# The activations' two halves placed behind the weights' slots and the constants in a partition of SBUF

## What is computed

```python
mod = silu(c) @ w_ada + b_ada                  # six vectors of 2048
hn = modulated_rms_norm(h, sh1, sc1)
proj = hn @ w_in                               # 2048 x 5664: attention q/k/v, DeltaNet q/k/v, z, b, a
attn_out = axial_gqa_attention(...)            # 8 heads, 2 kv heads
dn_out = bidir_gated_deltanet(...)             # 8 heads, chunks, both directions
h = h + gt1 * (concat(attn_out, dn_out) @ w_out)
hn = modulated_rms_norm(h, sh2, sc2)
u = dwconv_centred(hn @ w_up, w_ffn_conv) + b_ffn_conv      # 2048 x 11264
h = h + gt2 * ((silu(u_gate) * u_val) @ w_down)             # 5632 x 2048
return rms_norm(h) * final_norm
```

## Time and profile before

| | |
|---|---|
| median of 3 runs | 2742.33 us (2741.33 to 2742.73) |
| the profiled execution's own time | 2742.49 us |
| its span, first to last instruction | 2739.5 us |
| TensorE: matmul instructions busy | 2580.1 us of the span, 12198 instructions |
| VectorE / ScalarE busy | 1430.4 us / 1018.2 us |
| mean granted TensorE clock | 0.977 |

### The profile page before, as it was taken

How to read it: one execution, slowest core, us unless ns; L and a number is a source line. 1 busy time by engine, 2 the same in 40 slices (tenths; PEclk the granted TensorE clock), 3 DMA queues, 4 the chain that set the end, 5 groups by cost and what they waited for, 6 DMA issues and landing times.

```text
span 2739.5 us, 35454 instructions
## 1 busy us (share of the span) xinstructions
PE 2580.1 (94%) x12198; PEld 2093.2 (76%) x12198; DVE 1430.4 (52%) x1846; ACT 1018.2 (37%) x1422; POOL 189.5 (7%) x270
## 2 busy tenths in 40 slices
PE   2589999999999989997999999999999999999997
PEld 1467877878778768785888888887888888888885
DVE  5835666666666654445444434444344444444554
ACT  4124343343443443434444234443234432222334
POOL 2200211211211201100000000000000000000000
PEclk9689999999999999999999999999999999999998
DMA  9835434445445422432333333333333333333233
GB/s 338 299 106 155 139 111 143 138 115 146 131 116 151 132 62 70 123 98 59 96 92 90 95 106 92 95 97 90 97 96 99 92 90 94 100 100 99 85 90 123
DMA packets 436095, 318.42 MB, mean 116 GB/s; under 512 B 12582, under 2 KB 408657, under 8 KB 435537
## 3 DMA queue, kind: packets, MB, share of 16 engines
q1 hardware_dynamic: 406192, 212.19, 27.0%
q0 software_dynamic: 28928, 104.87, 12.0%
q10 hardware_dynamic: 929, 0.74, 0.1%
HBM read 313.56 MB, written 4.19 MB: 116 GB/s over the span
## 4 chain that ended last, share of the span: by engine, by line
PE 85%; DVE 6%; ACT 3%; DMA 3%; issue 2%; DVEq 0%; ACTq 0%; POOLq 0%
PE pw L1307 22%; PE pw L1309 21%; PE pw L1308 21%; PE pw L1291 2%; PE pw L1292 2%; PE pw L1293 2%; PE pd L1525 2%; PE pd L1548 1%; PE pd L1561 1%; DMA DD<-in_w_ada_dram 1%; DMA T<-in_w_ada_dram 1%; PE pd L1508 1%; PE pd L1568 1%; DVE act L1014 1%; DVE PTb L864 1%
## 5 line engine op out<-in xcount | busy, mean ns | idle before, releaser
L1307 PE MATMUL pw<-act_hi,w_hi 128*128 128x512 f32 x2048 | 832.9, 407 | 17.2 <-DVE act_lo L1202 9.2
L848 DVE TENSOR_TENSOR w_lo<-raw,w_hi 128x1024 fp32r<-128x1024 f32 x426 | 520.6, 1222 | 548.1 <-ACT w_hi L502 546.4
L1309 PE MATMUL pw<-act_hi,w_lo 128*128 128x512 f32 x2048 | 800.7, 391 | 0.0
L1308 PE MATMUL pw<-act_lo,w_hi 128*128 128x512 f32 x2048 | 798.7, 390 | 0.0
L502 ACT ACTIVATE w_hi<-raw 128x1024 fp32r<-128x1024 f32 x426 | 450.3, 1058 | 526.4 <-PE pw L1309 440.8
L1307 PEld LDWEIGHTS pw<-act_hi,w_hi 128*128 128x128 f32 x2048 | 385.7, 188 | 112.0 <-issue 23.3
L1309 PEld LDWEIGHTS pw<-act_hi,w_lo 128*128 128x128 f32 x2048 | 385.2, 188 | 83.2
L1308 PEld LDWEIGHTS pw<-act_lo,w_hi 128*128 128x128 f32 x2048 | 386.3, 189 | 78.6 <-issue 7.2
L1307 PE MATMUL pw<-mh_hi,w_hi 128*128 128x512 f32 x704 | 280.3, 398 | 1.1 <-DVE w_lo L848 1.1
L1308 PE MATMUL pw<-mh_lo,w_hi 128*128 128x512 f32 x704 | 278.3, 395 | 0.0
L1309 PE MATMUL pw<-mh_hi,w_lo 128*128 128x512 f32 x704 | 278.3, 395 | 0.0
(11 more groups left out here) (265 smaller groups left out, 2562.0 us busy)
## 6 DMA issues: line engine op xcount, KB each, us to landing
raw<-in_w_up_dram SPq DMA_DIRECT2D x176, 512.0 KB, 4.1
ada_w<-in_w_ada_dram POOLq DMA_DIRECT2D x128, 512.0 KB, 4.4
raw<-in_w_in_dram SPq DMA_DIRECT2D x88, 512.0 KB, 3.9
raw<-in_w_down_dram SPq DMA_DIRECT2D x64, 384.0 KB, 3.5
raw<-in_w_down_dram SPq DMA_DIRECT2D x64, 320.0 KB, 3.2
raw<-in_w_out_dram SPq DMA_DIRECT2D x32, 512.0 KB, 4.4
DD<-in_w_ada_dram POOLq DMA_DIRECT2D x16, 512.0 KB, 6.0
EG<-in_w_ada_dram POOLq DMA_DIRECT2D x16, 512.0 KB, 5.4
```

The source lines that it names most:

```text
L848: V.tensor_tensor(w_lo[slot][:], raw[slot][:], w_hi[slot][:].bitcast(F32), ALU.subtract).then_inc(lo_made.sem, 1)
L1307: M(bank, w_hi[slot][:, k, :], hi[:, k0 + k, :], start=first, stop=False)
L1308: M(bank, w_hi[slot][:, k, :], lo[:, k0 + k, :], start=False, stop=False)
L1309: ins = M(bank, w_lo[slot][:, k, :], hi[:, k0 + k, :], start=False, stop=last)
```

## The change

The lines that allocate `act_hi`, `x_feat`, `otok` and `act_lo` are moved from the front of the list to behind `nrm`. Nothing else is edited: on each of the five engines the program has the same instructions in the same order.

```diff
-        act_hi = sb("act_hi", [P, KT, S], F32R)
-
-        for_float32 = ExitStack()
-        x_feat = sb("x_feat", [P, KT, S], F32, for_float32)
-        for_float32.close()
-        otok = sb("otok", [P, NB, DM], F32, for_float32)
-        for_float32.close()
-        act_lo = sb("act_lo", [P, KT, S], F32R)
         raw = [sb(f"raw{i}", [P, UK, P]) for i in range(2)]
         w_hi = [sb(f"w_hi{i}", [P, UK, P], F32R) for i in range(2)]
         w_lo = [sb(f"w_lo{i}", [P, UK, P], F32R) for i in range(2)]
...
         nrm = sb("nrm", [P, 3, NB])
+        act_hi = sb("act_hi", [P, KT, S], F32R)
+
+        for_float32 = ExitStack()
+        x_feat = sb("x_feat", [P, KT, S], F32, for_float32)
+        for_float32.close()
+        otok = sb("otok", [P, NB, DM], F32, for_float32)
+        for_float32.close()
+        act_lo = sb("act_lo", [P, KT, S], F32R)
```

## The result

The changed kernel takes 2777.16 us (median of 4 runs, 2774.8 to 2779.2), the kernel before 2741.83 us in the same comparison: ratio 1.013, 95% interval 1.0116 to 1.0144. It is 35.3 us slower. The profiled execution has a span of 2774.3 us, 34.8 us more than before.

The account below looks back on a forecast made before the run. TensorE was taken to bound the kernel; up parts 27.9, heads 5.0, output projection 3.2 and start 1.0 made 37.1 us on 2742.3, rounded to 2779.5 us. The forecast's own range was 2774 to 2785, widened to 2770 to 2791.

Parts of the forecast that it names:

- The pitch: Up parts: act's matmuls go from 226.7 to mh's 233.3 ns, 6.67 ns more each, 27.9 us over 4176 matmuls.
- 33 pieces of 64 bytes: Moving operand's read: 2048 bytes take 32 pieces from a multiple of 64, 33 from elsewhere; one more is 16 cycles.
- So it is not the weights: Changeover from up to down part: weight load is 0.19 us on both sides, so weights do not cause the 6.67 ns.
- The short pieces: Heads: six matmuls cost nothing more, nine 0.015 us, later ones 6.67 ns each; 0.42 us a head, 5.0 together.
- the rival with the steady price everywhere: First rival: short pieces also pay 6.67 ns a matmul; heads 14.6 us, total 47.6 us, 2790 us; chance 0.14.
- the start: Before the heads: 144 of 240 act matmuls pay, the others' price is covered; 1.0 us, bounds 0 and 1.6.
- the output projection: Behind the last head: 527 matmuls at 6.67 ns, 3.5 us, less some 0.3 for seven starts; 3.2 us.
- VectorE's and ScalarE's new addresses: Writing and reading act at its new addresses: taken as 0, upper bound 0.4 us.
- High addresses: Second rival: the price belongs to high addresses, not the remainder; 0 to 12 us, 2742 to 2755; chance 0.05.
- the down part's shorter units: Part of the third rival: units of 6 and 5 blocks make the down part's pitch; 2742 us; rival's chance 0.13.
- "no change": Third rival: the change costs nothing, as the page's 16-byte rule would have it; 2742 us, chance 0.13.
- The fourth: Rival: new distance between weights and activations removes a 13.3 ns read conflict; 2649 us, or about 2700 with both; chance 0.03.

Follow-up runs that it names:

- The separate kernel: A kernel computing nothing of the reference, running matmul streams and short pieces in or out of step; nine matmuls took 2.139 us in step, 2.171 at 224 apart.
- the first three runs: Changed kernel with act 32 bytes on, 2740.98 us; kernel before with act 32 bytes on, 2777.51 us; kernel before with mh 32 bytes on, 2728.53 us.
- the 57 placements: Different placements in a kernel of 59 streams of 48 matmuls, weights or moving operand shifted; 226.7 ns in step, 228.9 to 237.9 ns out of step.

## Why the prediction was right, and where its reason was not

**The pitch.** Right in size and place. The forecast took 233.3 ns for `act` from the down part, and the up parts have it to the digit. The step that carried it is the sentence on low address bits: "any rule that looks at low bits alone must give the up part the pitch of the down part". That argument needed no mechanism, and it covers the true rule, since it kept the low bits of the weights and of the activations both, and with them the distance.

**The mechanism.** The 33 pieces of 64 bytes were wrong. "So it is not the weights", concluded from a weight load of 0.19 us on both sides, was the failing step: the load's own length says nothing of whether the weights' address sets the pitch. Moving the weights alone by 32 bytes costs as much in the up part as moving the activations, and moving both costs nothing. The coincidence of 6.67 ns with 16 columns was what made the story look complete.

**The short pieces.** The forecast priced a head at 0.42 us instead of 1.6. The six inner heads went from 104.65 to 104.96 us each (mean distance between the same instruction of one and the next), 0.3 more; the whole stretch cost 4.2 us where 5.0 stood, and the rival with the steady price everywhere 14.6. In both traces the pieces can be laid side by side, from a piece's first start to the next operation's. On the mean of the six inner heads a piece of 3 costs 2.5 ns more, one of 6 costs 7 (nothing was forecast for both), one of 9 costs 12.5 (15), one of 12 costs 31 (35) and one of 15 costs 56 (55). Of the two pieces of 18 (75 each) one costs 64; the other becomes 88 ns shorter. That one holds two waits for VectorE, before (first two lines) and after:

```profile
479.12 0.50 PE L1307 MATMUL pw<-act_hi,w_hi 128*128 128x512 f32 x1 [0.73 <-DVE w_lo L848]
483.53 1.13 PE L1486 MATMUL pd<-act 128*128 128x128 f32 x8 [1.39 <-DVE act L1030]
...
481.00 0.50 PE L1307 MATMUL pw<-act_hi,w_hi 128*128 128x512 f32 x1 [0.61 <-DVE w_lo L848]
485.41 1.13 PE L1486 MATMUL pd<-act 128*128 128x128 f32 x8 [1.34 <-DVE act L1030]
```

Together they shrink from 2.10 to 1.95 us on the mean of the six heads, so part of what the other pieces pay is made up there. This is what the forecast of the heads left out. The separate kernel does not carry over: nine matmuls pay 32 ns in it, and priced by its table a head would pay some 0.8 us (an estimate). Why the same pieces pay less in the head isn't shown.

**The sum.** 37.1 us against 34.8 in the span. Besides the heads, the terms that were too large are the start (1.0, measured -0.3) and the output projection (3.2, measured 2.9). The start can't be read to a microsecond: in the twelve traces of the real kernel in its layouts the first matmul of the heads starts anywhere from 192.2 to 195.6 us. Two counts in the sum are off: of the 768 matmuls at lines 1291 to 1293 the last head moves 240, not 264, and 528, not 527, follow it, which is worth under 0.2 us. VectorE's and ScalarE's new addresses cost nothing that shows. The end is 0.3 us longer, but not by the change: it takes 23.1 us in the trace before and 23.3 to 23.4 in each of the eleven others, those in step among them.

**The rivals.** High addresses, the down part's shorter units and "no change" are excluded by the first three runs. The fourth, with a chance of 0.03, had the right cause, a pitch that depends on how far apart weights and activations lie, and the wrong consequence for this change, a gain. What stood against it holds: `act_hi` gets the very distance that `mh_hi` has, so it can't gain. Of the 57 placements none is faster than in step. The Trainium skill, in SBUF — State Buffer (section "SBUF: two separate sides"), gives SBUF cachelines of 16 bytes, by which any multiple of 16 is the start of a line. That rule does not set the price here: 32 bytes, a multiple of 16, cost 1.3%, and both operands shifted by 16 together went from 226.7 to 231.1 ns, by 32 together did not.

**What stays open.** Why 256 bytes, why the out-of-step price is there at 512 moving columns and not at 384 or 256, why a narrower weight load in step is slower than a full one, and what the 13.3 ns in every matmul are. So is why the short pieces pay less in the heads than in the separate kernel. The runs show that the pitch depends on both operands' addresses; that two reads collide in banks of SBUF would be a guess.

## What to carry to other kernels

Where TensorE is the bound and streams float32r blocks of 512 columns, with a load of 128 columns of weights before each, look at the difference of the first bytes of the weights' and the activations' tensors, for each half. In these runs a multiple of 256 bytes was best, with each at a multiple of 32. Here one pad of 32 bytes gave 0.4%, and an innocent reordering of allocations took 1.3%. Read the pitch from starts, for each stage and each operand; two pitches for one shape of matmul may be a gain, as the down parts' 12 us were here. And an argument by "the same low bits as a case that the trace shows" is safer than the mechanism that one likes.

## What the runs showed of the hardware that I had not expected

- The pitch of 128x512 float32r matmuls depends on the distance between weights and moving operand modulo 256 bytes: 226.7 ns in step (both at multiples of 32), 228.9 to 237.9 ns otherwise, worst with the moving operand moved by 4 bytes. Full-float32 matmuls (429 ns for 512 columns, 112 ns for 128) do not.
- In step, the pitch is the columns' time at 2.4 GHz and 13.3 ns: 120.0, 173.3 and 226.7 ns at 256, 384 and 512 columns.
- Weight loads of 32 or 64 columns instead of 128 did not speed such a stream up in step: 231.7 and 230.0 ns, against 226.7. At 224 apart they did a little: 230.0 and 231.7 against 233.3.
- The first matmul of a float32r piece behind full-float32 ones of at most 128 columns has its successor 312 to 322 ns later, in the kernel before and in the changed one; behind ones of 512 columns it is 330 to 639 ns.
